# Head norms from columns of sums, and D's input factor as a product

## The reference

```python
def _l2_norm(x):
    return x * lax.rsqrt(jnp.sum(x * x, axis=-1, keepdims=True) + NORM_EPS)

# branch A: q, k (1, 1024, 4, 128) after a causal convolution and silu
aq = _l2_norm(aq.reshape(B, S, GDN_HEADS, GDN_HEAD_DIM)) * (GDN_HEAD_DIM ** -0.5)
ak = _l2_norm(ak.reshape(B, S, GDN_HEADS, GDN_HEAD_DIM))
ao = _gated_delta_rule(aq, ak, av, g, beta)
ao = _rms_norm(ao, a_norm_g).reshape(B, S, BRANCH_WIDTH)
y_a = ao * jax.nn.silu(a_z)

# branch D
log_a = -LRU_C * r * jax.nn.softplus(-lam)
a = jnp.exp(log_a)
bterm = jnp.sqrt(-jnp.expm1(2.0 * log_a)) * (ig * xf)     # then h_t = a_t h_{t-1} + bterm_t

# each branch: merged += sigmoid(gates_n) * (y_n @ w_br[n])
```

## Time and profile before

| | |
|---|---|
| median of three runs | 3804.34 us |
| the profiled execution, on the device | 3806.69 us |
| its span in the profile | 3804.8 us |
| mean granted TensorE clock | 0.956 |
| TensorE, VectorE, GpSimd, ScalarE busy | 91%, 48%, 42%, 24% |

### The profile page before, as it was taken

One profiled execution on the slowest core, in us unless ns is written; L12 is line 12 of the kernel. 1 busy time (PEld: TensorE's weight loads), 2 busy tenths in 40 slices (PEclk: granted clock), 3 DMA queues, 4 the chain that ended last, 5 costly groups with the idle time before them and its releaser, 6 DMA issues.

```text
span 3804.8 us, 43576 instructions
## 1 busy us (share of the span) xinstructions
PE 3445.9 (91%) x16228; PEld 2768.2 (73%) x16228; DVE 1826.8 (48%) x2464; ACT 915.7 (24%) x1745; POOL 1585.7 (42%) x2013
## 2 busy tenths in 40 slices
PE   7998999989978999979899999888859989999988
PEld 6777888867756667767677677777747767678767
DVE  4765343356883545643523647465543443212343
ACT  3233222230122432323112222222211122210021
POOL 3544742235763234533454344344314434334423
PEclk9999999999989999989899999999979999999999
DMA  3122321122212011131121210000102101111211
GB/s 113 50 67 62 94 76 45 56 69 63 67 58 75 20 40 58 44 97 34 49 94 42 70 39 28 23 28 28 28 11 86 46 27 45 50 54 36 81 36 67
DMA packets 300660, 205.32 MB, mean 54 GB/s; under 512 B 25749, under 2 KB 277657, under 8 KB 300473
## 3 DMA queue, kind: packets, MB, share of 16 engines
q1 hardware_dynamic: 271241, 132.77, 12.8%
q10 hardware_dynamic: 29232, 69.95, 5.0%
HBM read 173.06 MB, written 29.63 MB: 53 GB/s over the span
## 4 chain that ended last, share of the span: by engine, by line
PE 59%; DVE 15%; ACT 3%; POOL 2%; issue 2%; PEld 1%; ACTq 1%; DMA 1%; PEldq 0%; DVEq 0%; POOLq 0%
PE ps L343 46%; PE ps L889 4%; DVE wrk L753 3%; PE ps L1426 2%; ACT wrk L917 2%; PE ps L902 1%; POOL w_lo L2720 1%; PE ps L1832 1%; POOL w_hi L2715 1%; DVE wrk L942 1%; PEld ps L2229 1%; PE ps L2203 1%; DVE small L945 1%; PE ps L779 1%; DVE wrk L732 1%
## 5 line engine op out<-in xcount | busy, mean ns | idle before, releaser
L2715 POOL TENSOR_TENSOR w_hi<-w_raw,pool_one 128x256 fp32r<-128x256 f32 x1004 | 689.5, 716 | 2166.1 <-PE ps L343 2114.8
L343 PE MATMUL ps<-h_hi,w_hi 128*128 128x512 f32 x2928 | 1208.1, 413 | 84.3 <-POOL w_lo L2720 24.4
L343 PE MATMUL ps<-h_hi,w_lo 128*128 128x512 f32 x2928 | 1154.7, 394 | 0.0
L343 PE MATMUL ps<-h_lo,w_hi 128*128 128x512 f32 x2928 | 1154.4, 394 | 0.0
L2720 POOL TENSOR_TENSOR w_lo<-w_raw,w_hi 128x256 fp32r<-128x256 f32 x1004 | 897.1, 923 | 23.1
L343 PEld LDWEIGHTS ps<-h_hi,w_hi 128*128 128x128 f32 x2928 | 558.6, 191 | 261.4 <-issue 102.0
L343 PEld LDWEIGHTS ps<-h_hi,w_lo 128*128 128x128 f32 x2928 | 557.2, 190 | 121.4
L343 PEld LDWEIGHTS ps<-h_lo,w_hi 128*128 128x128 f32 x2928 | 559.7, 191 | 113.4 <-issue 9.6
L343 PE MATMUL ps<-y_hi,w_hi 128*128 128x512 f32 x704 | 290.9, 413 | 31.2 <-issue 30.4
L343 PE MATMUL ps<-y_hi,w_lo 128*128 128x512 f32 x704 | 277.8, 395 | 0.0
L343 PE MATMUL ps<-y_lo,w_hi 128*128 128x512 f32 x704 | 277.5, 394 | 0.0
(11 more groups left out here) (357 smaller groups left out, 3824.9 us busy)
## 6 DMA issues: line engine op xcount, KB each, us to landing
w_raw<-in_w_in SPq DMA_DIRECT2D x87, 512.0 KB
w_raw<-in_even_w_in SPq DMA_DIRECT2D x48, 512.0 KB
away<-wrk ACTq DMA_DIRECT2D x80, 256.0 KB, 2.0
wrk<-away ACTq DMA_DIRECT2D x32, 512.0 KB
w_raw<-in_odd_w_in SPq DMA_DIRECT2D x32, 512.0 KB
wrk<-in_x ACTq DMA_DIRECT2D x16, 512.0 KB, 8.7
w_raw<-in_w_br SPq DMA_DIRECT2D x32, 256.0 KB
w_raw<-in_even_w_out SPq DMA_DIRECT2D x24, 256.0 KB
```

What stands on the lines that cost most here:

```text
L343: mm = nc.tensor.matmul(ps[:, b, 0:n], w[:, slot, k, :], rhs(part, k, b), start=(k == 0 and q == 0), stop=(k == nk - 1 and q == 2))
L2715: ins = nc.gpsimd.tensor_tensor(hi, raw, one[:, 0:2], ALU.mult)
```

## The change

In `head_norm` the squares become the weights: for each 128 positions a product with one column of ones gives the sums as a column (position on the partition), four columns for a half tile. ScalarE takes the root of 128x4, VectorE inverts 128x4, and TensorE spreads the four columns with the identity over all partitions, into the same PSUM bank, from which VectorE multiplies. The planned times of the two norms go from 80 to 30 and from 44 to 16. In D the factor 1 - a*a was 2 t / (1 + t) with t = tanh; it becomes t (1 + a*a), with a at hand in `wt(2)`, and its stage goes from 13 to 5.

```diff
-    def head_norm(name, tile, n, scale, factor, sq=4, rs=6, us=80.0, ready=None):
+    def head_norm(name, tile, n, scale, factor, sq=4, rs=6, us=30.0, ready=None):
...
-        N = 2 * n + 2
+        N = 2 * n + 3.2
+        rows = lambda i: wt(rs, 0)[:, 8 * (i % 4):8 * (i % 4) + 4]
+        inverse = lambda i: wt(rs, 0)[:, 8 * (i % 4) + 4:8 * (i % 4) + 8]
+
+        def in_turn(*steps):
+            for at, i, do in sorted(((i + lag, i, do) for lag, do in steps for i in range(2 * n)),
+                                    key=lambda e: e[:2]):
+                yield at / N
+                do(i)
 
         def f_act(act):
...
+            def root(i):
+                act.wait_ge(summed.sem, summed.nth(i))
+                if i >= 4:
+                    act.wait_ge(inverted.sem, inverted.nth(i - 4))
+                nc.scalar.activation(rows(i), ps[:, 2 + i % 4, 0:4], ACT.Sqrt, bias=EPS,
+                                     scale=scale).then_inc(rooted.sem, 1)
+            yield from in_turn((0.0, square), (1.2, root))
 
         def f_pe(pe):
-            for i in range(2 * n):
-                yield (i + 0.1) / N
+            def sums(i):
                 pe.wait_ge(squared.sem, squared.nth(i))
                 if i >= 4:
-                    pe.wait_ge(root.sem, root.nth(i - 4))
-                nc.tensor.matmul(ps[:, 2 + i % 4, :], ones, wt(sq, i % 2), start=True,
-                                 stop=True).then_inc(summed.sem, 1)
+                    pe.wait_ge(normed.sem, normed.nth(i - 4))
+                for c in range(4):
+                    mm = nc.tensor.matmul(ps[:, 2 + i % 4, c:c + 1], wt(sq, i % 2)[:, c * P:(c + 1) * P], ones[:, 0:1],
+                                          start=True, stop=True)
+                mm.then_inc(summed.sem, 1)
+
+            def columns(i):
+                pe.wait_ge(inverted.sem, inverted.nth(i))
+                for c in range(4):
+                    mm = nc.tensor.matmul(ps[:, 2 + i % 4, c * P:(c + 1) * P],
+                                          inverse(i)[:, c:c + 1].to_broadcast([P, P]), ident, start=True, stop=True)
+                mm.then_inc(spread.sem, 1)
+            yield from in_turn((0.3, sums), (1.9, columns))
 
         def f_dve(dve):
-            ch = chains["dve"]
-            for i in range(2 * n):
-                yield (i + 2.1) / N * 0.999
-                dve.wait_ge(root.sem, root.nth(i))
-                ch.link(nc.vector.reciprocal(wt(rs, i % 2), wt(rs, i % 2)))
+            def invert(i):
+                dve.wait_ge(rooted.sem, rooted.nth(i))
+                if i >= 4:
+                    dve.wait_ge(spread.sem, spread.nth(i - 4))
+                nc.vector.reciprocal(inverse(i), rows(i)).then_inc(inverted.sem, 1)
+
+            def scaled(i):
+                dve.wait_ge(spread.sem, spread.nth(i))
                 x = tile(i // 2, i % 2)
-                nc.vector.scalar_tensor_tensor(x, x, factor(i // 2), wt(rs, i % 2), ALU.mult,
+                nc.vector.scalar_tensor_tensor(x, x, factor(i // 2), ps[:, 2 + i % 4, :], ALU.mult,
                                                ALU.mult).then_inc(normed.sem, 1)
+            yield from in_turn((1.5, invert), (3.0, scaled))
...
-    o_normed = head_norm("A norm out", a_tile, 4, 1.0 / P, lambda j: col("a_norm_g"), sq=8, rs=9, us=44.0)
+    o_normed = head_norm("A norm out", a_tile, 4, 1.0 / P, lambda j: col("a_norm_g"), sq=8, rs=9, us=16.0)
...
-            ch.link(nc.vector.tensor_scalar(wt(0), wt(3), 1.0, None, ALU.add))
-            for b in range(2):
-                yield 0.1 + 0.3 * b
-                nc.vector.reciprocal(wt(0, b), wt(0, b))
-            yield 0.7
-            dve.drain()
-            nc.vector.scalar_tensor_tensor(wt(3), wt(3), 2.0, wt(0), ALU.mult, ALU.mult)
+            ch.link(nc.vector.tensor_tensor(wt(0), wt(2), wt(2), ALU.mult))
+            ch.link(nc.vector.scalar_tensor_tensor(wt(3), wt(0), 1.0, wt(3), ALU.add, ALU.mult))
             nc.vector.tensor_tensor(wt(1), wt(1), wt(8), ALU.mult)
-        stage("D input factor", 13.0, dve=dt_dve)
+        stage("D input factor", 5.0, dve=dt_dve)
```

More of the change, by code:

```diff
@@ L690, in part_ready @@
         return lambda pe, k, b: pe.wait_ge(parted.sem, parted.nth(b * KD + k))
-    def head_norm(name, tile, n, scale, factor, sq=4, rs=6, us=80.0, ready=None):
+    def head_norm(name, tile, n, scale, factor, sq=4, rs=6, us=30.0, ready=None):
         squared = sig.take("hn_squared", 2 * n)
         summed = sig.take("hn_summed", 2 * n)
-        root = sig.take("hn_root", 2 * n)
+        rooted = sig.take("hn_rooted", 2 * n)
+        inverted = sig.take("hn_inverted", 2 * n)
+        spread = sig.take("hn_spread", 2 * n)
@@ L698, in head_norm @@
         normed = sig.take("hn_normed", 2 * n)
-        N = 2 * n + 2
-        def f_act(act):
[L702 to L709, removed]
-                if i >= 2:
[L711 to L716, removed]
+        N = 2 * n + 3.2
@@ new lines, in head_norm, with square @@
+        rows = lambda i: wt(rs, 0)[:, 8 * (i % 4):8 * (i % 4) + 4]
[5 more added lines that the diff above has]
+                do(i)
+        def f_act(act):
+            def square(i):
+                if ready and i % 2 == 0:
+                    act.wait_ge(*ready(i // 2))
+                if i >= 2:
+                    act.wait_ge(summed.sem, summed.nth(i - 2))
+                nc.scalar.activation(wt(sq, i % 2), tile(i // 2, i % 2), ACT.Square).then_inc(squared.sem, 1)
+            def root(i):
[5 more added lines that the diff above has]
+            yield from in_turn((0.0, square), (1.2, root))
```

## The result

The changed kernel takes 3819.93 us (median of 10 runs, 3813.57 to 3824.95) against 3803.59 us before, beside it (10 runs): ratio 1.0039, interval 1.0029 to 1.0049, **16.3 us slower**. 3812 was said for the median, slower, within 3790 to 3828: the direction and the range held, the value was 8 us low. That it came so near is partly luck: behind it lie two terms that were wrong by some 7 and 11 us in opposite directions, and both lay outside the bounds that were given for them.

The account below looks back on a forecast made before the run. TensorE, busy for 91% of the span, was taken to bound the kernel. 3 + 7 - 1.5 = +8.5 on the profiled 3806.7 us gave 3815.2, said as 3812 for the median; own range 3807 to 3822, full range 3790 to 3828.

Parts of the forecast that it names:

- First norm, +3: First head norm: narrow products cost TensorE more than the removed waits give back; +3 us, from -2 to +6.
- the step: Both norms: one set of narrow sums and spreads on TensorE, put at 2.05 us (1.78 to 2.2) against 0.86.
- 2.5 us of stall at the ends: First norm: TensorE stall expected to remain at both ends after the change, 2.5 us.
- "nothing": Eight chunks behind the first norm: density of wide parts kept, so no change; up to 3 us without cover for table loads.
- Second section, +7: Second norm and B branch: a hold of +18 us, then -11 us behind it; +7 us, from -6 to +17.
- 17 (894 against 877): A merge's second pair: L469 comes at about 894, behind six taps, while TensorE could have had the pair at 877.
- -11: From the second merge pair through the layer norm: 235 us against 246.1, so -11 us (-6 to -14).
- D, -1.5: Branch D's factor: 4.3 us less wait inside the D merge against +2.8 in the rounds; -1.5 us, -5 to +4.
- +2.8: D's rounds: about 29 us of TensorE against a chain of 30; waits up to 2 us in each of three rounds.
- rival 3: The clock: narrow steps leave TensorE at its lower level for half of the 24, 3836; with rival 4, chance 0.15.
- Rival 1: Second section: the six taps don't hold TensorE, second merge pair within 3 us of 875.8; 3789, chance 0.20.
- rival 4: Norm steps not overlapped as written, each waiting 1 us for root and inverse, 16 more: 3828; with rival 3, chance 0.15.

Follow-up runs that it names:

- the run alone: Only the first norm narrow and planned at 30, second norm and D as in the kernel before: 3798.15 us, ratio 0.9987.
- conv_planned_late: Changed kernel with B glu's fetch planned at 42 instead of 14, so the B convolution is planned at 64 as before: 3813.96 us, ratio 1.0027.
- norms_out44: Kernel before with both norms narrow, D as before, the second norm keeping its planned 44: 3799.88 us, ratio 0.9990.
- the pair of runs above: Both norms narrow, D old, convolution planned late: second norm planned at 16 with fetch at 42 (3805.07 us), or at 44 (3799.88 us).

## Why the prediction was right or wrong

- **First norm, +3; the section shows -3.8, the run alone -5.** The mechanism held: TensorE paces the norm, and the wide products beside it are moved, not saved. The term that failed is the step, taken at 2.05 us from its own form in the Roots helper; it measured 1.78, the lower bound, that is 4.3 us over 16 steps. The 2.5 us of stall at the ends weren't there either (0.2). The chunks aren't quite the "nothing" that was said: they took 1.6 us more, but with 19 wide products more in them, 4.4 us of work, which then didn't follow the last chunk.
- **Second section, +7; +8.0.** Taps ahead of A z's gates hold TensorE: that was said and came, and the sum was right partly by luck. The second pair starts 16.5 us later, counted from the norm's first sums. conv_planned_late splits this: 12.5 go with the taps, where the reckoning had 17 (894 against 877), and 4.0 are there without them, where it had about 1: that kernel's first steps have no wide work among them (norms_out44, which has, starts the pair at 81.4). The wait that was named was the wrong one: I followed L469 alone, but the long wait ended with the last gate and the sigmoid behind it, and L469 had 0.90. Behind the hold -11 was said and 250.8 against 259.3 us, -8.5, came: the tap tail took 69.7 us (said 70), the layer norm's wait fell from 10.4 to 3.2 us, but its sums now wait 5.6 us for ScalarE where they waited 1.3.
- **D, -1.5; +9.7.** This is the term that made the forecast low, and it lies outside its own bounds of -5 to +4. The gain was sized right, 16.82 to 12.77, -4.05 against -4.3. The rounds were put at +2.8 by comparing two lengths, 29 us of TensorE and a chain of 30; GpSimd was in neither, and the plan's shorter round was taken as harmless to it. I had weighed the contention with GpSimd for the convolution, "a few us", and not for the one place where the change swaps one-operand operations for two-operand ones. The whole stretch cost 9.7; with the 4.05 taken back, and 1.55 more at the wait behind the merge (3.99 to 5.54), the rounds cost 12.2. These are TensorE's waits for GpSimd, 14.0 instead of 5.1, its waits for VectorE, 0.9 instead of 2.4, and 4.8 us more of busy time for the same 586 records (149.95 against 145.12), at a granted clock of 0.92 instead of 0.93.
- **The clock**, rival 3: it asked for half of the 24 steps at the lower level. What came is six sets of sums and four of spreads, the first ones of the second norm; the pair of runs above prices the unmixed order at 3.5 to 5.2 us. In the first norm the granted clock was 1.00. Rival 1 (the taps don't hold) and rival 4 (no overlap) are excluded by the rows around 880 and by the first norm without waits.
- **The sum.** -3.8 + 8.0 + 9.7, with -0.3 between them and 1.5 from the start, is 15.1 us in the profiles (16.3 in the medians) where +8.5 was said: the first norm was put 7 too high, D 11 too low.

## What to carry to other kernels

When a planned order takes a stage's cost as its input, a cheaper operation and its new cost are two changes: try the operation at the old cost first. Here the two old costs were worth 18 us, with the same arithmetic. Before replacing a slow one-operand VectorE operation, look which GpSimd work lies beside it and who waits for that. A wait marked "issue" is followed to the engine whose instruction ends just ahead of it, not to the one expected.

## What the hardware showed that was not expected

- Four fp32 sums with one moving column take 0.81 us, four spreads with 128 columns 0.97: the moving columns hardly count, and the eight narrow products of a step with their loads (1.78) cost twice one fp32 product of 512 columns (0.86).
- TensorE without any gap, on narrow fp32 products alone, was granted 0.50 in 794 to 807, after a wait of 3.87 us at 790; a step took 3.41 us. After the same wait (3.86 us), but with wide products among the steps, norms_out44 was granted 1.00 from 800 on, and in the first norm, where wide products lie among them too, a step took 1.78 us.
- GpSimd's split of one tile: 5.2 to 5.6 us beside reciprocals, 10.6 beside operations with two SBUF operands, 15.96 beside taps with hardly a pause.
